# A two-layer hybrid backbone: the first layer's early sort of the latents, the additions within the last up product, the first expert's other banks, and more unread products

## The reference

```python
def ec_moe(h, router, w_up, w_down):
    cap = CAPACITY_FACTOR * T // N_EXPERTS          # 64 of 512 latents, 32 of 256 context tokens
    aff = jax.nn.softmax((h @ router), axis=-1)
    gate, idx = lax.top_k(jnp.swapaxes(aff, 1, 2), cap)   # each of 16 experts picks its tokens
    xg = h[bidx, idx]
    up = jnp.einsum('becd,edf->becf', xg, w_up)
    hid = jax.nn.silu(up[..., :D_EXPERT]) * up[..., D_EXPERT:]
    y = jnp.einsum('becf,efd->becd', hid, w_down) * gate[..., None]
    return jnp.zeros_like(h).at[bidx, idx].add(y)
...
for i in range(2):
    x = x + g1 * mixer_i(...)        # layer 0: recurrent mixer, layer 1: latent attention
    x = x + g2 * ec_moe(modulate(rmsnorm(x, norm_ffn[i]), s2, sc2), ...)
    # in layer 0 the same for ctx
return rmsnorm(x, norm_final)
```

## Time and profile before

| what | value |
|---|---|
| median of 3 runs | 1851.48 us (1850.93 to 1858.81) |
| the profiled execution | 1851.95 us, its span 1850.2 us |
| TensorE matmul busy | 1678.3 us (91%) |
| VectorE, ScalarE, GpSimd busy | 709.5, 524.5, 180.4 us |
| transfers | 520.54 MB, mean 281 GB/s |
| mean granted TensorE clock | 0.972 of full |

### The profile page before, as it was taken

How to read it: one execution, slowest core, us unless ns; L and a number is a source line. 1 busy time by engine, 2 the same in 40 slices (tenths; PEclk the granted TensorE clock), 3 DMA queues, 4 the chain that set the end, 5 groups by cost and what they waited for, 6 DMA issues and landing times. The chain is left out here.

```text
span 1850.2 us, 23812 instructions
## 1 busy us (share of the span) xinstructions
PE 1678.3 (91%) x9749; PEld 875.3 (47%) x9749; DVE 709.5 (38%) x1426; ACT 524.5 (28%) x881; POOL 180.4 (10%) x196
## 2 busy tenths in 40 slices
PE   4999989769999999999988999999959998888887
PEld 2767668533333333333358778877733332222222
DVE  4667765431122221221145655666451221122113
ACT  4677783201111110110144445436210000000002
POOL 1000010100001001000011324324000000000001
PEclk8999999989999999999989999999969999999999
DMA  9554351799999999999881000001579999999996
GB/s 358 190 205 163 146 219 58 277 366 410 391 405 397 396 404 391 398 405 386 312 303 63 24 1 0 0 0 54 207 288 418 420 421 421 421 422 420 421 422 252
DMA packets 89576, 520.54 MB, mean 281 GB/s; under 512 B 11347, under 2 KB 19648, under 8 KB 33936
## 3 DMA queue, kind: packets, MB, share of 16 engines
q1 hardware_dynamic: 80128, 487.74, 65.4%
q0 software_dynamic: 9360, 31.54, 5.5%
HBM read 502.37 MB, written 16.88 MB: 281 GB/s over the span
## 5 line engine op out<-in xcount | busy, mean ns | idle before, releaser
L793 PE MATMUL wide<-sb_ring_x,sb_xT 128*64 128x512 f32 x1160 | 268.2, 604 | 22.2 <-DMA sb_ring_x<-moe_w_up 19.9
L793 PE MATMUL wide<-sb_ring,sb_xT 128*64 128x512 f32 x888 | 201.8, 597 | 15.4 <-DMA sb_ring<-moe_w_up 13.3
L793 PEld LDWEIGHTS wide<-sb_ring_x,sb_xT 128*64 128x64 f32 x1160 | 78.4, 138 | 196.3 <-issue 138.1
L793 PEld LDWEIGHTS wide<-sb_ring,sb_xT 128*64 128x64 f32 x888 | 60.4, 136 | 145.1 <-issue 107.1
L856 PE MATMUL duo<-sb_ring_x,sb_hidT 128*64 128x512 f32 x536 | 124.3, 599 | 4.4 <-DMA sb_ring_x<-moe_w_down 4.4
L1740 DVE TENSOR_TENSOR sb_hid<-wide,sb_sg 128x512 f32<-128x512 f32 x16 | 11.1, 692 | 302.7 <-ACT sb_sg_c L1290 302.7
L2150 POOL TENSOR_TENSOR sb_prob<-sb_prob,sb_asum 128x768 f32<-128x768 f32 x64 | 93.8, 1466 | 183.4 <-DVE sb_asum L1976 183.4
L856 PE MATMUL duo<-sb_ring,sb_hidT 128*64 128x512 f32 x424 | 100.1, 601 | 7.3 <-DMA sb_ring<-moe_w_down 7.3
L1740 DVE TENSOR_TENSOR sb_hid<-wide,sb_hid 128x512 f32<-128x512 f32 x16 | 11.1, 692 | 246.1 <-ACT sb_hid L1288 246.1
L1288 ACT ACTIVATE sb_sg<-wide 128x512 f32<-128x512 f32 x16 | 9.6, 597 | 338.0 <-PE wide L801 338.0
L1288 ACT ACTIVATE sb_hid<-wide 128x512 f32<-128x512 f32 x16 | 9.6, 597 | 280.5 <-PE wide L793 280.5
...
## 6 DMA issues: line engine op xcount, KB each, us to landing
...
```

What stands on the lines that cost most here:

```text
L793: ins = mm(wide[n * CAPL:(n + 1) * CAPL, s, :], mine[:, k, :], w[:, at:at + BANK], start=k == 0, stop=k == KD - 1)
```

## The change

1. **Early sort.** In layer 0 the logits, the softmax and four of the eight sort rounds of the latents (`EARLY_R`, on 32 rows) are done before the last context tile: three rounds ahead of `residual(0, s, 5)`, one behind `logits_sum(4)`. The context takes part from round 4 on. TensorE cuts the products of tiles 4 and 5 to turn logits and affinities between their pieces. ScalarE makes the exponentials twice and touches the square root between (`ACT.Sqrt` on one number).
2. The last `ada_chunk(4, 7)` stands behind the turn of the affinities, and `open_buffers(0)` behind `s_top`.
3. **Other banks.** The first expert of layer 0 turns its hidden rows into `duo`, and no longer waits for `s_xgT`.
4. **Additions.** In layer 1 the additions of the seventh pair stand inside the last `up`, and on VectorE ahead of `hidden(15)`.
5. **Unread products.** 32 become 46, 24 become 30, and 10 new ones stand behind the first turn of layer 1's gathered rows.
6. Two memsets on GpSimd at the start; some semaphores are joined.

```diff
+                    product(4, 0, 4)
+                    logit_products(2)
+                    turn_tile(s, 3)
+                    turn_logits(1)
+                    product(4, 4, KD)
+                    turn_logits(2)
+                    logit_products(3)
+                    product(5, 0, 1)
+                    turn_logits(3)
+                    product(5, 1, 4)
+                    pe.wait_ge(s_aff, 1)
+                    for half in range(2):
+                        ins = turn(turned[0:2 * E, 0, half * P:(half + 1) * P], aff2[:, half, 0:2 * E])
+                    ins.then_inc(s_afft, 1)
+                    product(5, 4, KD)
+                    pe.wait_ge(s_affl, 1)
+                    turn_tile(s, 4)
+                    pe.wait_ge(s_x1[0], n_t - 1)
+                    for k in range(4):
+                        ada_chunk(4, k, used[place[names[3]][0]] if k == 0 else None)
+                    logit_products(4)
+                    turn_tile(s, 5, used[Y_SLOT])
+                    turn_logits(4)
+                    ada_chunk(4, 4)
+                    logit_products(5)
+                    turn_logits(5)
+                    for k in range(5, 7):
+                        ada_chunk(4, k)
+                    return
...
             def turn_choice(lay):
-                pe.wait_ge(s_aff, lay + 1)
+                pe.wait_ge(s_aff, lay + 2)
                 for t in range(2):
                     ins = turn(turned[0:3 * E, 0, t * P:(t + 1) * P], aff2[:, t, :])
                 ins.then_inc(s_afft, 1)
+                if lay == 0:
+                    ada_chunk(4, KD - 1)
...
-                idle_products(wide[:, 3, :], 14 if lay == 0 else 24)
+                idle_products(wide[:, 3, :], 14 if lay == 0 else 30)
...
+                    if t == 0 and halves[0] == 0:
+                        pe.wait_ge(s_ylo, p + 1)
+                    for n in halves:
...
                                 ins.then_inc(used[place["up", lay, e, k][0]], 1)
+                            if lay == 1 and e == E - 1 and k >= 2:
+                                for j in ((k - 2,) if k < 6 else (2 * k - 8, 2 * k - 7)):
+                                    add_rows(E // 2 - 2, j // 2, (j % 2,))
...
+                    banks = duo if lay == 0 and e == 0 else turned
                     pe.wait_ge(s_hid, done + e + 1)
-                    pe.wait_ge(s_xgT, 2 * done + parts)
+                    if banks is turned:
+                        pe.wait_ge(s_xgT, 2 * done + parts)
...
-                        ins = turn(turned[:, 0, kk * P:(kk + 1) * P], hidn[lay][:, at:at + 2 * P - 1:2])
+                        ins = turn(banks[:, 0, kk * P:(kk + 1) * P], hidn[lay][:, at:at + 2 * P - 1:2])
...
-                                if e >= 2 and e % 2 == 0:
+                                if e >= 2 and e % 2 == 0 and e < E - 2:
                                     add_rows(e // 2 - 1, c)
...
+                if lay == 1:
+                    idle_products(wide[:, 3, :], 10)
                 up(0, True)
...
             turn_mods(5)
-            idle_products(duo[:, 0, :], 32)
...
+                    logits_out(2)
+                    modulate(s, 3)
+                    logits_out(3)
+                    squares(s, 4)
+                    affinities(0, TLT, 1)
+                    fn(mx[:, 3, 0:1], eps[:, 0:1], ACT.Sqrt)
+                    squares(s, 5)
+                    modulate(s, 4)
+                    logits_out(4)
+                    modulate(s, 5)
+                    logits_out(5)
+                    affinities(TLT, TT, 2)
+                    return
...
+            def shift_logits(t0, t1):
+                lg = logits[:, t0:t1, :]
+                chain.step(v.tensor_reduce(mx[:, 0, t0:t1], lg, AX_X, ALU.max))
+                v.tensor_tensor(aff[:, t0:t1, :], lg, mx[:, 0, t0:t1].unsqueeze(2).to_broadcast([P, t1 - t0, E]),
+                                ALU.subtract).then_inc(s_sub, 1)
...
+            def sort_round(r, rows):
...
+                chain.step(v.max(lists[rows, 1, at], affT[rows]))
+                chain.step(v.max_index(top_i[rows, at], lists[rows, 1, at], affT[rows]))
+                if r < CAPL // 8 - 1:
+                    chain.step(v.match_replace(affT[rows], lists[rows, 1, at], affT[rows], -1.0))
...
+                M = CAP[lay]
+                t0, t1 = (TLT, TT) if lay == 0 else (0, TLT)
+                shift_logits(t0, t1)
+                shares(t0, t1, lay + 2)
+                dve.wait_ge(s_afft, lay + 2)
+                new = slice(2 * E, 3 * E) if lay == 0 else slice(0, 3 * E)
+                chain.step(v.tensor_copy(affT[new], turned[new, 0, 0:2 * P]))
+                r0 = EARLY_R if lay == 0 else 0
+                for r in range(r0, CAPL // 8):
+                    sort_round(r, slice(0, 3 * E))
+                    if lay == 1 and r == 0:
+                        open_buffers(1)
                 chain.step(v.tensor_copy(lists[:, 0, :], top_i[:]))
                 chain.step(v.tensor_scalar(lists[:, 0, :], lists[:, 0, :], first[:, 0:1], None, ALU.add))
                 v.tensor_copy(lists[:, 2:4, :], lists[:, 0:2, ::-1]).then_inc(s_top, 1)
+                if lay == 0:
+                    open_buffers(0)
...
+                    add_pair(E // 2 - 2)
                     hidden(E - 1)
-                    add_pair(E // 2 - 2)
...
+                    residual(0, s, 4)
+                    logits_sum(2)
+                    normed_tile(s, 4)
+                    logits_sum(3)
+                    dve.wait_ge(s_logr, 4)
+                    shift_logits(0, TLT)
+                    shares(0, TLT, 1)
+                    dve.wait_ge(s_afft, 1)
+                    v.tensor_copy(affT[0:2 * E], turned[0:2 * E, 0, 0:2 * P]).then_inc(s_affl, 1)
+                    dve.wait_ge(s_affl, 1)
+                    for r in range(EARLY_R - 1):
+                        sort_round(r, slice(0, 2 * E))
+                    residual(0, s, 5)
+                    modulate(s, 4)
+                    normed_tile(s, 5)
+                    modulate(s, 5)
+                    logits_sum(4)
+                    sort_round(EARLY_R - 1, slice(0, 2 * E))
+                    logits_sum(5)
+                    dve.wait_ge(s_logr, 6)
+                    return
...
+            g_.memset(lists[:], 0.0).then_inc(s_const, 1)
+            g_.memset(top_i[:], 0).then_inc(s_const, 1)
```

236 lines of the change are left out of this document (124 added, 112 removed).

## The result

| | before | changed |
|---|---|---|
| median time, us (12 runs each) | 1852.21 (1850.14 to 1858.81) | 1845.21 (1841.15 to 1848.52) |
| ratio, 95% interval | | 0.9962 (0.9953 to 0.9970) |
| profiled execution, time and span | 1851.95, 1850.2 | 1847.21, 1845.5 |

A forecast was written before the change was run, and what follows sets the result against it. TensorE bounds layer 0's experts, transfers layer 1's, with serial stretches ahead and between. Terms 6.75 + 2.0 + 1.2 + 2.2 + 1.5 - 0.2 = 13.45 us give 1838.0 against the median; 8 in 10 for 1833.5 to 1845.5.

The forecast's parts named there:

- the case given 0.14: Whole kernel: the time can't be told from no change, within 0.5% or 9.3 us; chance 0.14.
- Early sort, up to the issue of the gather: Layer 0's choice: lists done 7.75 us earlier, so the gather is issued at 370.95 instead of 378.70.
- Issued while the first expert's chunks still flow, I take 8.8: Layer 0's gather: 8.8 us from issue to landing; bounds 7.8 and 12.5.
- The rival "the gather gives it back": Layer 0: gather lands 12.5 us after issue, gaining 3.1, and the clock costs 2.9: 1844.6; chance 0.2.
- The term of 6.75: Layer 0, sort through gather: 6.75 us gained by the earlier sort; bounds 3.1 and 7.75.
- First expert's banks, 2.0: Layer 0's first experts: without the wait, the next up product starts 2.0 us earlier; gain 2.0, from 0.9 to 2.6.
- Unread products at layer 1's start, 1.2: Layer 1's first turn and product: 14 more unread products keep the clock up; gain 1.2 us, between 0.8 and 2.6.
- Unread products at layer 1's experts, 2.2: Layer 1's first up product: at full clock it releases slots sooner, transfers flow earlier; gain 2.2 us, bounds 0.7 and 2.9.
- Additions, 1.5: End of layer 1's experts: moved additions let the last down product start earlier; gain 1.5 us, between 1.0 and 2.7.
- Memsets, -0.2: Kernel start: two memsets of 0.1 to 0.2 us ahead of GpSimd's first transfers; loss 0.2 us.
- Table switches: Layer 0's softmax on ScalarE: each switch holds it twice 1.28 us; 1.8 less gained, 1839.8; chance 0.03.
- the late store: Layer 0: last normed tile's store lands near 385, delaying merge and gather; gather 8.8 us later, time 1853.6; chance 0.03.

The follow-up runs named there:

- five chunks held: The changed kernel with five chunks of the first expert's up weights held back until the gather has landed: 1836.95 us, ratio 0.9918.
- sort_only: The kernel before with the early sort alone (and the two memsets): 1848.50 us, ratio 0.9974.

## Why the prediction was wrong

The direction held and the time, 1845.2, lay at the upper edge of the range, but the gain was half the one forecast, and the case given 0.14, within 0.5%, came. By its steps:

- *Early sort, up to the issue of the gather.* Right, with one slip: the items of the cut product add up to 2.2 us and not 2.4, and the sixth residual moved by 2.0. Residual 348.75 for 349.1, rounds ahead of it, affinities turned at 360.59 for 361.1, gather issued at 370.17 for 370.95.
- *"Issued while the first expert's chunks still flow, I take 8.8".* This step failed. I took the latency of two gathers that were issued later in layer 0; it was 10.2 and 11.3 us (up to 12.7 in other kernels), since here it was issued into a backlog of eight chunks. The product started 5.2 us earlier in the mean of the profiles, instead of 6.75. And the term left out the clock: I wrote 2.9 us for it in a rival, where it belonged in the sum. I tied it there to the longer gap ahead of a late gather; with five chunks held that gap was gone and the clock fell all the same, so the link between the early sort and the clock is shown, its cause is not. Measured over the unfilled profiles: 1.9 us in the first up product and, against the kernel before, 1.0 in the second. The term of 6.75 came to about 2.3. (`sort_only` gave 2.0 to 7.6 us by its interval, 4.7 by the medians, so it agrees only just.)
- *The rival "the gather gives it back"* (chance 0.2, 1844.6; 1841 for the clock alone) is what happened; its 12.5 us was the nearer row to price the gather by (11.8 in the mean of nine profiles). That its 1844.6 lies so near the measured time is in part luck: it took the gather and the clock too dear together (0.2 left of the term, for 2.3) and the terms of layer 1's start and of the additions too high.
- *First expert's banks, 2.0.* Right: from the group at 400.03 to the second up product lie 17.63 us before and 15.65 after: 1.98, and the same within 0.25 in every profile. That the clock could fall there too was inside the term's bounds, and it did.
- *Unread products at layer 1's start, 1.2.* Too high for the changed kernel: about 0.5. The turn ran at full clock, the product behind it did not in either profile. With the same unread products it did in four of eight profiles, and with the 32 of before in none of six; at full clock that product is worth some 2 us more.
- *Unread products at layer 1's experts, 2.2.* Right in mechanism, 0.4 too low: from the start of the up product to SyncE's third transfer behind it 5.4 us in twelve profiles with them, 7.1 to 8.4 in six without.
- *Additions, 1.5.* Mis-sized: 0.7 by the profiles, and nothing that the times can tell. The text had the reason, the last chunk's arrival, and put too little weight on it: the last down product now waits twice for a transfer.
- *Memsets, -0.2.* GpSimd's transfers behind them start 0.36 us later (4.44 for 4.08); what reaches TensorE is lost in the spread of the profiles (layer 0's third residual at 308.45 for 308.31, and from 307.4 to 308.9 in others).

With the measured sizes, and the memsets as forecast, the sum is 2.3 + 2.0 + 0.5 + 2.6 + 0.7 - 0.2 = 7.9 us, against 7.0 measured. *Table switches* and *the late store* did not happen: the early load ended at 340.95 and its exponential waited 0.36 us more for VectorE alone, the second load ended at 359.65 and its exponential started at 359.66; and VectorE did not wait in `open_buffers(0)`.
